# Two more tile pairs of a projection as seven-product blocks, with the state tables packed into fewer tiles

## What is computed

```
h = rms_norm(x)                                   # 2048 x 1024
proj = h @ w_in                                   # 1024 -> 68 tiles of 128 columns
u_ssm(6) z_ssm(6) q(6) k(6) v(6) z_attn(6) q_mem(4) z_mem(4) gates(24)   # tiles of proj
y = s5_ssm(u_ssm)       # 48 groups, 64 complex states each, causal scan with tables
                        # (powers, input and output matrices, angles) from lambda, dt, B, C
o_ssm = gelu/GLU(y) * silu(z_ssm)
o_attn = dilated_window_attention(q, k, v, bias) * alpha * silu(z_attn)      # 12 heads
o_mem = softmax(q_mem @ k_mem^T) @ v_mem * silu(z_mem)                       # 4 heads, 256 memories
merged = sum over 3 branches of sigmoid(gates) * (branch @ w_branch)
x = x + merged @ w_out;  return rms_norm(x)
```

## Time and profile before

| | us |
|---|---|
| median of 3 runs | 2365.92 |
| lowest and highest | 2365.56, 2367.65 |
| the profiled execution, its own time | 2367.38 |
| its span, first to last instruction | 2365.6 |
| PE busy in the span | 2336.1 (99%) |
| DVE busy | 1798.3 (76%) |
| ACT busy | 790.1 (33%) |
| POOL busy | 287.7 (12%) |
| mean granted TensorE clock | 0.996 of full speed |

### The profile page before, as it was taken

One profiled execution on the slowest core, in us unless ns is written; L12 is line 12 of the kernel. 1 busy time (PEld: TensorE's weight loads), 2 busy tenths in 40 slices (PEclk: granted clock), 3 DMA queues, 4 the chain that ended last, 5 costly groups with the idle time before them and its releaser, 6 DMA issues.

```text
span 2365.6 us, 32904 instructions
## 1 busy us (share of the span) xinstructions
PE 2336.1 (99%) x12142; PEld 1894.9 (80%) x12142; DVE 1798.3 (76%) x3225; ACT 790.1 (33%) x1633; POOL 287.7 (12%) x400
## 2 busy tenths in 40 slices
PE   9999999999999999999999999999999999999998
PEld 8888888888887776787777777888888888888887
DVE  7457887787688879867787877788676777786875
ACT  6222212222243334335555575444552011110101
POOL 0421111111001111110000000111100000000000
PEclk9999999999999999999999999999999999999999
DMA  8444354344475577544444474688755866758471
GB/s 336 149 117 132 91 144 144 123 141 131 122 218 180 177 251 222 179 134 169 139 143 134 160 278 148 214 289 274 250 204 181 267 178 186 227 178 246 147 245 54
DMA packets 193811, 431.70 MB, mean 182 GB/s; under 512 B 29295, under 2 KB 74451, under 8 KB 184180
## 3 DMA queue, kind: packets, MB, share of 16 engines
q1 hardware_dynamic: 154036, 273.32, 37.2%
q0 software_dynamic: 38576, 154.19, 19.0%
q10 hardware_dynamic: 1040, 2.10, 0.2%
HBM read 283.38 MB, written 146.11 MB: 182 GB/s over the span
## 4 chain that ended last, share of the span: by engine, by line
PE 94%; DVE 2%; DMA 2%; ACT 1%; issue 1%; SPq 0%; DVEq 0%; ACTq 0%
PE bank L138 28%; PE bank L140 27%; PE bank L139 27%; PE bank L2914 2%; PE bank L2935 1%; PE bank L2957 1%; PE bank L2809 1%; PE bank L2893 1%; PE bank L2823 1%; PE bank L2826 1%; PE bank L2871 1%; DMA w_raw<-w_br 1%; PE bank L2945 1%; DMA sign<-sign_c 1%; DVE h_lo L2343 1%
## 5 line engine op out<-in xcount | busy, mean ns | idle before, releaser
L138 PE MATMUL bank<-h_hi,w_hi 128*128 128x512 f32 (+1 forms) x2320 | 925.3, 399 | 16.0 <-DVE h_lo L2343 13.7
L140 PE MATMUL bank<-h_hi,w_lo 128*128 128x512 f32 (+1 forms) x2320 | 902.7, 389 | 0.0
L139 PE MATMUL bank<-h_lo,w_hi 128*128 128x512 f32 (+1 forms) x2320 | 901.5, 389 | 0.0
L138 PEld LDWEIGHTS bank<-h_hi,w_hi 128*128 128x128 f32 x2320 | 436.5, 188 | 116.5 <-issue 29.5
L140 PEld LDWEIGHTS bank<-h_hi,w_lo 128*128 128x128 f32 x2320 | 436.2, 188 | 92.2
L139 PEld LDWEIGHTS bank<-h_lo,w_hi 128*128 128x128 f32 x2320 | 436.8, 188 | 87.9 <-issue 1.7
L138 PE MATMUL bank<-h_hi 128*128 128x512 f32 (+1 forms) x704 | 270.2, 384 | 2.2 <-issue 1.1
L140 PE MATMUL bank<-h_hi,h_lo 128*128 128x512 f32 (+1 forms) x704 | 264.2, 375 | 0.0
L139 PE MATMUL bank<-h_lo,h_hi 128*128 128x512 f32 (+1 forms) x704 | 264.0, 375 | 0.0
L138 PEld LDWEIGHTS bank<-h_hi 128*128 128x128 f32 x704 | 132.5, 188 | 31.1 <-issue 8.2
L140 PEld LDWEIGHTS bank<-h_hi,h_lo 128*128 128x128 f32 x704 | 132.5, 188 | 24.3
(11 more groups left out here) (303 smaller groups left out, 2949.9 us busy)
## 6 DMA issues: line engine op xcount, KB each, us to landing
w_raw<-w_in SPq DMA_DIRECT2D x154, 256.0 KB, 4.4
gt<-proj_d POOLq DMA_DIRECT2D x32, 768.0 KB, 7.8
proj_d<-ev POOLq DMA_DIRECT2D x22, 1024.0 KB, 6.4
proj_d<-ev POOLq DMA_DIRECT2D x81, 256.0 KB, 4.7
proj_d<-keep POOLq DMA_DIRECT2D x79, 256.0 KB, 4.5
lo_raw<-hx_d SPq DMA_DIRECT2D x18, 1024.0 KB, 8.0
w_raw<-w_br SPq DMA_DIRECT2D x32, 512.0 KB, 4.5
wx_raw<-w_br SPq DMA_DIRECT2D x32, 512.0 KB, 4.2
```

What stands on the lines that cost most here:

```text
L138: nc.tensor.matmul(out, ah, bh, start=(start and n == 0), stop=False, skip_group_check=onto)
L139: nc.tensor.matmul(out, ah, bl, start=False, stop=False, skip_group_check=onto)
L140: last = nc.tensor.matmul(out, al, bh, start=False, stop=(stop and n == len(pairs) - 1), skip_group_check=onto)
```

## The change

Eight edits in one file.

1. `N_Z` goes from 28 to 24: the 4 tiles of q_mem leave the plain loop and form 2 pairs (`QUERY`) of seven-product blocks. `NBK` goes from 40 to 44. `block_at` now reads a list `ORDER`, in which the two query pairs stand behind the gate pairs. `finish` gets a branch that copies.
2. The tables start at tile 3 (`N_TAB`), and `table_steps` gives the 88 steps of the first 11 units to 76 chunks (22 steps on 19 chunks), the last unit one step a chunk on tiles 22 and 23. Some chunks carry two steps.
3. `pair_slot`: a pair of groups every six half steps in place of four.
4. `B0` goes from 128 to 160, and the loads and gelus at the end of the blocks (`LOAD_Y`, `GELU`) by 32.
5. SP waits, ahead of the first memory queries, for the stores of all query blocks (`queries_kept`).
6. In SP's block loop the load of an exchanged operand stands ahead of the weight loads, and three of the weight loads one step later.
7. In ACT's block loop the rounding of an exchanged operand (`operand_hi`) stands at the end of the fourth step behind the product (it stood in the fifth, ahead of the side work); in DVE's, `operand_lo` stands in the fifth step ahead of the side work (it stood behind it).
8. POOL makes two quarters of operands beside tiles 4 and 5, and is done by tile 21.

```
-        N_VAL, N_TAB, N_Z, N_GATE = 6, 4, 28, 44
+        N_VAL, N_TAB, N_Z = 6, 3, 24
...
-        N_SILU = (N_GATE - N_Z) // 2
+        N_QM, N_SILU = 2, 8
...
+        SILU, QUERY, GATE = (range(N_QM, N_QM + N_SILU), range(N_QM), range(N_QM + N_SILU, NPAIRS))
+        ORDER = ([(p, (3, 2)) for p in SILU] + [(p, (1, 0)) for p in (*reversed(SILU), *GATE, *QUERY)]
+                 + [(p, (3, 2)) for p in (*reversed(QUERY), *reversed(GATE))])
...
-        def table_step(n, c):
-            u, part = divmod(n - N_TAB, 2)
-            return u, 4 * part + c
+        N_FAST = 4 * (N_Z - 2 - N_TAB)
+        FAST_STEPS = 8 * (NU - 1)
+        def table_steps(n, c):
+            t = 4 * (n - N_TAB) + c
+            if 0 <= t < N_FAST:
+                steps_in = range(-(-t * FAST_STEPS // N_FAST), -(-(t + 1) * FAST_STEPS // N_FAST))
+            elif t >= N_FAST and n < N_Z:
+                steps_in = (FAST_STEPS + t - N_FAST,)
+            else:
+                steps_in = (-1,) if t == -1 else ()
+            return [divmod(x, 8) for x in steps_in]
...
-        P_PAUSE, PAUSE = 13, 0
         def pair_slot(p):
-            return S0 + 2 * p + (PAUSE if p >= P_PAUSE else 0)
+            return S0 + 3 * p
...
-        B0 = 128
+        B0 = 160
...
+                def queries_kept():
+                    blocks = N_SILU + NPAIRS + N_QM
+                    sp.wait_ge(c11_stored, 16 * blocks)
+                    sp.wait_ge(c21_stored, 16 * blocks)
+                    for i in range(2):
+                        sp.wait_ge(c12_stored[i], 16 * blocks // 2)
+                        sp.wait_ge(*count(c22_stored[i], 16 * blocks // 2))
...
                     if beat == A_END + 3:
                         sp.wait_ge(o_mm, NT_B)
+                        queries_kept()
                         for i in range(2):
-                            sp.wait_ge(stored[i], 16 * (N_Z // 2))
                             load_queries(i)
...
                 for v in range(N_STEPS):
                     row, at = divmod(v, NPR)
-                    if at == 0 and row + 1 < NBK:
-                        load_a11(row + 1)
-                    if at == 1 and row + 1 < NBK and row + 1 not in AGAIN:
-                        load_a12(row + 1)
-                    if at == 4 and row + 2 < NBK and row + 2 not in AGAIN:
-                        load_a21(row + 2)
-                    if at == 6 and row + 2 < NBK and row + 2 not in AGAIN:
-                        load_a22(row + 2)
                     if v and product_at(v - 1) is not None and product_at(v - 1)[0] in SWAPS:
                         b, i = product_at(v - 1)
                         sp.wait_ge(*count(mul_done, MADE[v - 1]))
                         load_operand(stage_of(b) + 1, i)
+                    if at == 0 and row + 1 < NBK:
+                        load_a11(row + 1)
+                        if row and row + 1 not in AGAIN:
+                            load_a22(row + 1)
+                    if at == 2 and row + 1 < NBK and row + 1 not in AGAIN:
+                        load_a12(row + 1)
+                    if at == 5 and row + 2 < NBK and row + 2 not in AGAIN:
+                        load_a21(row + 2)
...
-                    for swap in SWAPS:
-                        done = product_at(v - 5) if v >= 5 else None
-                        if done is not None and done[0] == swap:
-                            operand_hi(stage_of(swap) + 1, done[1])
...
+                    done = product_at(v - 4) if v >= 4 else None
+                    if done is not None and done[0] in SWAPS:
+                        operand_hi(stage_of(done[0]) + 1, done[1])
...
+                    done = product_at(v - 5) if v >= 5 else None
+                    if done is not None and done[0] in SWAPS:
+                        operand_lo(stage_of(done[0]) + 1, done[1])
...
-                    for swap in SWAPS:
-                        done = product_at(v - 5) if v >= 5 else None
-                        if done is not None and done[0] == swap:
-                            operand_lo(stage_of(swap) + 1, done[1])
```

43 lines of the change are left out of this document (24 added, 19 removed).

## The result

The changed kernel takes **2413.19 us** (median of 5 runs, 2409.77 to 2418.9), the kernel before 2366.99 in the same comparison. The ratio is 1.0197, 95% interval 1.0186 to 1.0209: 46.2 us slower, where 7.4 were predicted, and outside the range of 2349 to 2383 us. The sign was right, the size was not. The profiled execution took 2414.53 us with a span of 2412.6, 47.0 more than the span before.

A forecast was written before the change was run, and what follows sets the result against it. PE was taken as the bound throughout. Products -10.9, exchanges -9.7, packed tables +27 and seams +1 sum to +7.4 us on 2367.38, 2374.8; with the median 1.5 lower, 2373.3 us, range 2349 to 2383 (8 in 10).

The forecast's parts named there:

- Part 1, products: Memory-query tiles: 112 triples in place of 128, 0.68 us each, new DVE and ACT work hidden: -10.9 us.
- Part 2, exchanges: Exchanged operands: earlier load, rounding and rest remove most of PE's 13.7 us of waits for DVE: -9.7 us.
- leave 4 of 13.7: Exchanges: nearly all the first one's waits go; 4 us stay because the second falls into attention again.
- nothing is gained in total, 0: Exchanges, the term's unfavourable end: the second gets worse for the other beats it meets, 0 us gained.
- Part 3, tables packed: Table stage: eleven rounds fall short of the packed slots and PE waits: +27 us, from 10 to 36.
- The ring of DVE, SP's stores and ACT: Table stage: each unit's round passes through these engines in turn and takes 41.7 us, 41.5 kept, against 38.5 offered.
- the signs named: Profile after: PE waits for ACT's copies or `ca`, ACT waits longer, DVE stops waiting for PE at the splits.
- the rate: Table stage: a round needs 41.5 us, 38.5 are offered; short by 3.0 us each, 33 us over 11 rounds.
- 5.4 us to spare: Table stage: ACT's copy of a chunk can be this late before PE needs its bank; used up once, then PE waits.
- Part 4, seams: First scan, last unit, first memory queries and start of attention: together +1 us, from 0 to 6.
- The rule of the skill: ACT's table load: 2.66 us per switch with its drain, estimated 15 us more; the row gave nothing more and decided.
- The exchanges keep their waits, and the seams show: Rival: the second exchange gains 0 and the seams cost 5 us, giving 2387 us; chance 0.09.

The follow-up runs named there:

- the last version at full size: Changed kernel with operand sums on DVE, SP sending parameters, cosines, response in that order, scans over sooner, memory attention a half step later: 2366.43 us.
- one pair of tiles: Changed kernel with one query pair in blocks instead of two, operand sums on DVE, SP sending parameters, then cosines, then response: 2366.93 us.
- narrow sums: Changed kernel with POOL's operand sums two columns wide instead of 512 from the second group on, output not right: 2378.19 us.
- the one with the filler: Changed kernel with idle 128 by 128 matmuls ahead of the response product of units 0, 1, 6, 8 and 10: 2412.27 us.
- the sums on DVE: Changed kernel with the 64 operand sums of 128 by 512 made by DVE instead of POOL: 2397.39 us.
- the two edits on the ring: Changed kernel, each edit run alone: operand sums on DVE instead of POOL, 2397.39 us; SP sending parameters, cosines, response in that order, 2398.86 us.
- the scans': Changed kernel with scans spaced eleven quarters of a half step instead of twelve, the last pair done twelve half steps earlier: 2404.38 us.
- all three: Changed kernel with operand sums on DVE, SP sending parameters, cosines, response in that order, and scans over sooner: 2370.80 us.
- the last versions: Changed kernel with DVE sums, parameters first, scans sooner, memory attention a half step later: 2366.43 us; the same with double slots at steps 6 and 7: 2373.18 us.

## Why the prediction was right or wrong

**Books of the runs**: packing 44.9, exchanges -0.6, products -10.9 (by count), start of the attention 9.3, queries 3.7 (the gain of the later memory attention), together 46.4 against 46.2 measured. The agreement within 1 us is luck. The parts come from kernels that differ in more than the part, and three of them are not what the changed kernel's own trace has: packing is 41 there by the place of unit 11's product, the exchanges gained 4.7 us of waits, and the products are worth less than their count.

**Part 1, products, -10.9: count right, worth too large, about 7.** There are 48 matmuls fewer, and DVE's and ACT's work for the new blocks is hidden but for the 1.0 us of a copy. But in the last version at full size (2366.43 us) PE's busy time is only 3.2 us below that of the kernel before, with 4.0 more of the clock's loss, so at most 7.2 of the 10.9 are there; with one pair of tiles it is at most 3.5 of 5.4 (1.7 and 1.8). The step was to price a block's triple like a plain tile's. What the timelines offer in its place is the side work between the products: the last matmul ahead of it takes 0.32 us to the next start and the first behind it 0.34, in place of 0.23 (at 1209.40 and 1202.68 us of the kernel before), so each interruption costs some 0.2 us. Behind the response product of unit 11 I count 148 interruptions in the kernel before and 165 in that version, since the scans and the new blocks spread them, and 17 x 0.2 = 3.4 us. That is an estimate from the starts, and no run tests it.

**Part 2, exchanges, -9.7: wrong, about 0 alone.** The row of 13.7 us was right and the edit did take most of `h_lo` (to 6.5 here, 5.8 alone). The step that failed was to leave 4 of 13.7 without asking who is second. `tsc` stood next in line, in the attention that shares the second exchange. The end "nothing is gained in total, 0" was in the text and is what the run gave; in the changed kernel, where the exchange meets other beats, 4.7 us of waits went.

**Part 3, tables packed, +27: mechanism right, size wrong, 44.9 alone and 41 in the changed kernel.** This is the step that decided the miss. The ring of DVE, SP's stores and ACT was the cause, as read from the earlier trace rows, and the signs named were found: waits for `ca`, DVE no longer waiting for PE. Three steps of the sum were off. The first is the rate. The response product of unit 11 comes 479.4 us behind that of unit 0. Eleven rounds of seven slots are 39.15 us each where nothing waits (422.26 to 461.41 above), and with some 11 us for the value copies (three rounds of about 48.4 us in place of 44.6 in the kernel before) that makes 442. So a round is short by 3.4 us, not 3.0, and eleven by 37 instead of 33. The second is the slack. The "5.4 us to spare" were ACT's, at the copy of a chunk; but PE pays at the response product, which stands behind DVE's matrices and had no spare left. The third is unit 0, which already waits 4.5 us. 37 + 4.5 = 42, and the place of unit 11's product says 41. For the packing alone the same sum is 39 + 5.1 = 44, of 44.9 measured.

What the round is made of was also read too kindly. In the unit of the earlier trace rows one step on the ring met a sum of POOL, 1.80 us of squaring for about 0.7. In the stretch DVE had 61 of 440 us in which it waited for PE, and what POOL took from it could hide there. I wrote that POOL holds DVE up "as before", since its share per round is the same. The share is, the cover is not: narrow sums gave 35.5 us, 3.2 a round.

There is a trap in this. PE's waits beside the tables come to 28.9 us, close to the 27 predicted, and looked like a hit. The run with the packing alone, the one with the filler and the place of unit 11's product show that 41 to 45 is the number: the half clock behind each wait is the rest of the same shortfall.

**Part 4, seams, +1 (0 to 6): wrong, 13 (9.3 and 3.7).** I had written that attention starts after its loads could land, which is true, and overlooked what is queued behind `groups_over` on SP: the weights of the block, for which DVE and then PE wait. The queries' wait was seen and held too small (3.2 us and the clock behind it).

**The clock: left out.** The earlier trace rows has a wait of 5.65 us, and the windows behind it in the kernel before,

```profile
1410.00:1420.00 10.00, 4.35 (x19) 3.33 (x19) 6.26 (x9) 9.37 (x25) 0.55 (x1) 0.93 1.02 404
1420.00:1430.00 10.00, 10.00 (x70) 7.95 (x70) 9.34 (x15) 6.41 (x18) 0.00 (x0) 0.73 0.26 97
```

were there to be read: a wait of that length costs more than its length. By the windows it adds 6.9 us here, in the two seams that the ring does not cover; some 2 of them lie inside the waits.

**The rule of the skill.** The Trainium skill, "ScalarE: Activation LUTs", What ACT_TABLE_LOAD costs, adds a drain to each load. The traces after agree with the row and not with it. In the changed kernel a load starts at 464.37 us, right at the end of the copy ahead of it, takes 1.28 us, and `sm_dt` follows at 465.66, 1.29 us behind the load's start.

**Rivals.** None came. "The exchanges keep their waits, and the seams show" (2387) had two of the misses, and a chance of 0.09; with the packing at 44.9, 18 us more, it would have said 2405. I let the two misses stand as one unlikely case, though each had a reason of its own to be likely.

**What stays open.** Why the sums on DVE give 16.1 us where narrow sums give 35.5 is explained only in rough, by their own 44 us on DVE (64 of 0.69) and by the waits for copies. In total time the two edits on the ring and the scans' should give 40.3 us (16.1, 14.9 and 9.3), and all three gave 42.9, a difference within what an excess carries. The share of the interruptions in the products' worth is an estimate. The wait of 4.4 to 4.8 us in unit 6 of the last versions starts where ACT stands more than 4 us for the store of a value tile; that was read from the trace, not tested.

## What to carry to other kernels

Before packing side work, add up how long the follower waits for the leader in the stretch (DVE for PE: 61 us in 440, 6.2 in a round of 44.6). That is the most room there can be: the change asked for 6.1 a round (44.6 to 38.5), so no margin was left for the waits on ACT and on the stores, and whatever hides in the room, another engine's interference included, comes onto the path. On a queue shared by the ring's transfers, send first what the ring waits for last: three calls in another order were worth 14.9 us. And if a wait goes, look at once for the next one behind it; here three of the gains (`h_lo` to `tsc`, cosines to parameters, matrices to copies with the sums on DVE) were handed on in part or in full.

## What the runs showed of the hardware

In this kernel a sum of 128x512 in 32 bits on POOL (1.30 us) stopped DVE for nearly all its length: narrow sums took 58 us off POOL and 51 off DVE. Operations with two input tensors were held, and also one with a single tensor (0.43 us, 2.76 beside two sums on end). DVE makes the same sum in 0.69 us, so handing work to POOL cost DVE more time than doing it: with the 64 sums on DVE its busy time was 12.6 us lower.

Behind PE's waits of 3.4 to 7.1 us beside the tables the matmuls started every 0.43 us in place of 0.23 for some 4 to 6 us, about 2 us of work lost each time; in unit 6 the clock fell 1.9 us before the wait was over. Filled with idle matmuls the clock stayed at 1.00. That was worth nothing where PE only follows another engine; where it leads, PE's busy time fell by 4.9 us together with the wait at the attention's start, as much as the clock's loss over the whole kernel fell.
